# Two-item rounds in the paired attentions of a 13-stage fp32 model kernel on Trainium2

## The reference, cut to what matters

```python
def masked_softmax(s, mask):
    s = jnp.where(mask, s.astype(jnp.float32), -jnp.inf)
    m = jnp.max(s, axis=-1, keepdims=True)
    e = jnp.where(mask, jnp.exp(s - m), 0.0)
    return e / jnp.sum(e, axis=-1, keepdims=True)

# nsa, 16 query heads on 4 groups: per head a selected and a window branch over causal keys, each times a gate,
# plus a compressed branch; moba, 16 heads: one causal attention per head (256 tokens are one block)
s = jnp.einsum('bhqd,bhkd->bhqk', q, k)
o = jnp.einsum('bhqk,bhkd->bhqd', masked_softmax(s, causal), v)
# na, 16 heads: 256 latent queries over 256 context keys and the 256 latent keys, with a bias
p = jax.nn.softmax(jnp.concatenate([s_ctx, s_lat + bias], -1), axis=-1)
o = jnp.einsum('bqhd,bkhd->bhqd', p, v_all)
out = o.reshape(b, s, 1024) @ w_o
```

## Time and profile before

| | |
|---|---|
| median of 3 runs | 2262.74 us (2260.32 to 2263.0) |
| the profiled execution | 2257.97 us, span 2256.2 us, mean granted clock 0.994 |
| busy: TensorE, its weight loads | 98%, 88% |
| busy: VectorE, ScalarE | 79%, 52% |
| chain that ended last | TensorE 85%, VectorE 9%, ScalarE 3%, DMA 1% |
| `nsa0` from its first scores to the end of its output product | 91 to 148.5 us |
| `moba0` | 423 to 453.9 us |
| `nsa1` | 1019 to 1075.7 us |
| `na0` | 1974 to 2031.9 us |

### The profile page before, as it was taken

The page is one execution under the profiler, slowest core; times in us unless marked ns, Lnnn a source line. Parts: engine busy times, 40 slices in busy tenths (PEclk is TensorE's granted clock), DMA queues, the critical chain, the costliest instruction groups (busy, mean ns, idle before and its releaser), DMA issues.

```text
span 2256.2 us, 38067 instructions
## 1 busy us (share of the span) xinstructions
PE 2206.5 (98%) x15324; PEld 1975.6 (88%) x15324; DVE 1786.5 (79%) x3510; ACT 1162.2 (52%) x2042; POOL 0.2 (0%) x4
## 2 busy tenths in 40 slices
PE   8999999999999999999999999999999999999998
PEld 7878889898889988896988887898888889989998
DVE  7788977789887798878798766577877876478888
ACT  4685554665553555458655634544222136376433
POOL 0000000000000000000000000000000000000000
PEclk9999999999999999999999999999999999999999
DMA  7416666356665566660566532024554523334563
GB/s 244 141 61 222 234 203 222 124 190 235 204 212 187 190 236 204 213 204 35 206 233 205 178 115 91 1 76 142 175 177 157 170 81 109 133 101 155 209 225 122
DMA packets 70160, 373.60 MB, mean 166 GB/s; under 512 B 7392, under 2 KB 16736, under 8 KB 37984
## 3 DMA queue, kind: packets, MB, share of 16 engines
q1 hardware_dynamic: 61472, 361.52, 47.1%
q10 hardware_dynamic: 8512, 9.63, 1.4%
HBM read 369.03 MB, written 1.05 MB: 164 GB/s over the span
## 4 chain that ended last, share of the span: by engine, by line
PE 85%; DVE 9%; ACT 3%; DMA 1%; issue 1%; ACTq 0%; DVEq 0%
PE ps L490 82%; DVE w_lo L1874 2%; DVE hid_f L2279 1%; DVE hid_f L2264 1%; DMA w_raw<-weights 1%; PE ps L860 1%; PE ps L771 1%; PE ps L843 1%; ACT w_hi L1252 1%; ACT hid_f L1456 1%; DVE v_sb L2379 0%; DVE X L2000 0%; DVE X L2147 0%; PE ps L759 0%; DVE a_both L1874 0%
## 5 line engine op out<-in xcount | busy, mean ns | idle before, releaser
L490 PE MATMUL ps<-a_both,w_hi 128*128 128x256 f32 (+1 forms) x4864 | 1058.2, 328 | 16.0 <-DVE a_both L1931 10.5
L490 PEld LDWEIGHTS ps<-a_both,w_hi 128*128 128x128 f32 x4864 | 809.4, 190 | 90.1 <-issue 14.5
L1874 DVE TENSOR_TENSOR w_lo<-w_raw,w_hi 128x1024 fp32r<-128x1024 f32 (+1 forms) x632 | 708.0, 1149 | 92.4 <-ACT w_hi L1252 85.7
L490 PE MATMUL ps<-a_both,w_lo 128*128 128x256 f32 (+1 forms) x3136 | 715.2, 292 | 0.0
L1252 ACT CAST w_hi<-w_raw 128x1024 fp32r<-128x1024 f32 (+1 forms) x448 | 414.8, 974 | 379.7 <-DMA w_raw<-weights 372.8
L490 PEld LDWEIGHTS ps<-a_both,w_lo 128*128 128x128 f32 x3136 | 521.9, 191 | 24.0
L490 PE MATMUL ps<-hid_both,w_hi 128*128 128x512 f32 (+2 forms) x2216 | 529.0, 348 | 4.9 <-DVE qk L2845 0.8
L490 PEld LDWEIGHTS ps<-hid_both,w_hi 128*128 128x128 f32 x2216 | 381.9, 189 | 59.3 <-issue 9.8
L490 PE MATMUL ps<-hid_both,w_lo 128*128 128x256 f32 (+2 forms) x1460 | 340.5, 305 | 0.0
L490 PEld LDWEIGHTS ps<-hid_both,w_lo 128*128 128x128 f32 x1460 | 236.5, 190 | 16.9
L1258 ACT CAST w_hi<-w_raw 128x1024 fp32r<-128x1024 f32 (+2 forms) x184 | 188.3, 1023 | 0.8 <-DMA w_raw<-weights 0.8
(11 more groups left out here) (235 smaller groups left out, 1906.2 us busy)
## 6 DMA issues: line engine op xcount, KB each, us to landing
w_raw<-weights SPq DMA_DIRECT2D x250, 1024.0 KB, 4.8
pe_sb<-weights SPq DMA_DIRECT2D x96, 512.0 KB, 5.6
w_raw<-weights SPq DMA_DIRECT2D x64, 704.0 KB, 4.0
pe_sb<-na_bias ACTq DMA_DIRECT2D x32, 128.0 KB, 2.2
X<-x_t SPq DMA_DIRECT2D x2, 512.0 KB, 6.9
X<-c_rows ACTq DMA_DIRECT2D x2, 512.0 KB, 4.1
qk<-qk ACTq DMA_DIRECT2D x4, 256.0 KB, 6.8
qk<-ctx_t ACTq DMA_DIRECT2D x1, 1024.0 KB, 5.3
```

Source lines behind the costliest of these rows:

```text
L490: return nc.tensor.matmul(out, stationary, moving, start=start, stop=stop)
L1874: return v.tensor_tensor(out, a, b.bitcast(F32), ALU.subtract)
```

## The change

TensorE's loop goes by rounds of two items: scores of 2j and 2j+1, turn of 2j-2, values of 2j-4 and 2j-3, turn of 2j-1. ScalarE copies item i-2 at step i, and takes the high parts of a round together at odd steps, ahead of the copy; VectorE takes the low parts at even steps, of items i-6 and i-5. The output product's parts are cut at 5 and 6 tiles (at 3 and 5 in `moba0`). `moba0` has room for seven turned tiles. The steps themselves become functions (`pair_scores`, `pair_turn`, `pair_values`, `pair_exps`, `pair_copy`, `pair_high`, `pair_reduce`, `pair_normalize`, `pair_low`) with the old bodies; `ada_tile` gets an argument and `MOBA_S`, `MOBA_T`, `MOBA_O` are defined, neither of which is used.

```diff
-        PAIR_SLOTS = 3
+        PAIR_SLOTS, MOBA_TURNED = 3, 7
...
+        def turned_slots(name):
+            return MOBA_TURNED if name == "moba0" else PAIR_SLOTS
...
@@ TensorE, pair_attention @@
-                for i in range(N + 3):
-                    if i < N:
-                        if i >= 2:
-                            pe.wait_ge(a["s_taken"], i - 1)
...
-                    beside(i)
-                    if i == N:
-                        out_part(range(0, 3))
-                    b = i - 2
-                    if 0 <= b < N:
-                        pe.wait_ge(a["p_ready"], b + 1)
-                        wait(pe, a["t_taken"], b)
...
-                    if i == N + 1:
-                        out_part(range(3, 5))
-                    b = i - 3
-                    if 0 <= b < N:
...
-                out_part(range(5, KD))
+                def turn(b):
+                    pe.wait_ge(a["p_ready"], b + 1)
+                    wait(pe, a["t_taken"], b)
+                    pair_turn(name, b, PAIR_T)
...
+                first, second = (5, 6) if N == 2 * KD else (3, 5)
+                for j in range(N // 2):
+                    for i in (2 * j, 2 * j + 1):
+                        if j > 0:
+                            pe.wait_ge(a["s_taken"], i - 1)
+                        pair_scores(name, i, PAIR_S[i % 2])
+                        beside(i)
+                    if j > 0:
+                        turn(2 * j - 2)
+                    if j > 1:
+                        values(2 * j - 4, 2 * j - 3)
+                    if j > 0:
+                        turn(2 * j - 1)
+                out_part(range(0, first))
+                turn(N - 2)
+                values(N - 4, N - 3)
+                turn(N - 1)
+                out_part(range(first, second))
+                values(N - 2, N - 1)
+                out_part(range(second, KD))
...
@@ ScalarE, pair_attention @@
-                for i in range(N + 3):
+                for i in range(N + 4):
                     if i < N:
...
-                    b = i - 1
-                    if 0 <= b < N:
-                        act.wait_ge(a["t_ready"], b + 1)
-                        if b >= PAIR_SLOTS:
-                            act.wait_ge(a["pv_done"], b - PAIR_SLOTS + 1)
...
+                    if i % 2 == 1:
+                        for b in (i - 5, i - 4):
+                            if 0 <= b and items[b]["last"]:
+                                pair_high(name, b, PAIR_O)
+                    if 0 <= i - 2 < N:
+                        pair_copy(name, i - 2, PAIR_T)
                     if behind:
                         behind(i)
-                    b = i - 3
-                    if 0 <= b and items[b]["last"]:
...
@@ VectorE, pair_attention @@
-                for i in range(N + 4):
+                for i in range(N + 5):
...
-                    b = i - 4
-                    if 0 <= b and items[b]["last"]:
...
+                    if i % 2 == 0:
+                        for b in (i - 6, i - 5):
+                            if 0 <= b and items[b]["last"]:
+                                pair_low(name, items[b]["tile"], PAIR_O)
```

More of the change, by code:

```diff
@@ new lines, in pair_copy, with pair_high @@
+            def pair_copy(name, b, banks):
+                act.wait_ge(att[name]["t_ready"], b + 1)
+                if b >= turned_slots(name):
+                    act.wait_ge(att[name]["pv_done"], b - turned_slots(name) + 1)
+                turned = ps[:, banks[0]:banks[1] + 1, 0:WIDTH[name]].rearrange("p r (n c) -> p r n c", c=HD)
+                nc.scalar.copy(t_pair(name, b).rearrange("p (n r c) -> p r n c", r=2, c=HD), turned).then_inc(att[name]["t_taken"], 1)
+            def pair_high(name, b, banks):
+                act.wait_ge(att[name]["pv_done"], b + 1)
+                t = ITEMS[name][b]["tile"]
+                nc.scalar.copy(a_hi[:, t, LAT], ps[:, banks[t % 2], 0:S]).then_inc(att[name]["o_hi"], 1)
@@ L1444, in pair_attention @@
             def pair_attention(name, beside=None, behind=None, load_bias=None):
-                a, items = att[name], ITEMS[name]
-                N, W = len(items), WIDTH[name]
-                for i in range(N + 3):
+                items = ITEMS[name]
+                N = len(items)
+                for i in range(N + 4):
                     if i < N:
[L1450 to L1458, removed]
+                        pair_exps(name, i)
@@ new lines, in pair_reduce @@
+            def pair_reduce(name, i, banks, bias=False):
+                a, W = att[name], WIDTH[name]
+                dve.wait_ge(a["s_ready"], i + 1)
+                if i >= PAIR_SLOTS:
+                    dve.wait_ge(a["t_ready"], i - PAIR_SLOTS + 1)
+                rows = ITEMS[name][i]["rows"]
+                for e in range(2):
+                    slot = 2 * (i % 2) + e
+                    if bias:
+                        dve.wait_ge(bias_loaded[slot], 16 * (i // 2 + 1))
+                    for r, (c, mask) in enumerate(rows):
+                        x = len(rows) * e + r
+                        last = v.tensor_tensor_reduce(p_pair(name, i)[:, e * W + c.start:e * W + c.stop], ps[:, banks[e], c],
+                                                      bias_ring[:, slot, :] if bias else mask, NEG_SCALE[name], 3e38,
+                                                      ALU.add, ALU.min, negmax[:, i % 4, x:x + 1])
+                last.then_inc(a["s_taken"], 1)
@@ new lines, in pair_normalize @@
+            def pair_normalize(name, b):
+                a, W = att[name], WIDTH[name]
+                rows = ITEMS[name][b]["rows"]
+                w = 2 * len(rows)
+                g = ITEMS[name][b]["gate"]
+                dve.wait_ge(a["exp_done"], b + 1)
+                step(v.reciprocal(recip[:, b % 4, 0:w], sums[:, b % 4, 0:w]))
+                if g is not None:
+                    sync()
+                    both = recip[:, b % 4, :].rearrange("p (e r) -> p e r", e=2)
+                    step(v.tensor_tensor(both, both, gate[:, :, g:g + REP + 1:REP].rearrange("p r e -> p e r"), ALU.mult))
+                sync()
+                for e in range(2):
+                    for r, (c, _) in enumerate(rows):
+                        at = p_pair(name, b)[:, e * W + c.start:e * W + c.stop]
+                        x = len(rows) * e + r
+                        last = v.tensor_scalar(at, at, recip[:, b % 4, x:x + 1], None, ALU.mult)
+                last.then_inc(a["p_ready"], 1)
```

120 lines of the change are left out of this document (57 added, 63 removed).

## The result

| | before | after |
|---|---|---|
| median | 2262.51 us (2257.71 to 2263.0, 5 runs) | 2272.2 us (2270.98 to 2275.31, 5 runs) |
| profiled execution | 2257.97 us, span 2256.2 | 2275.31 us, span 2273.5 |
| mean granted clock | 0.994 | 0.991 |

Ratio 1.0053, 95% interval 1.0042 to 1.0064. By these ratios the change costs 12 and 16 us; the medians lie 9.7 and 13.8 us apart. The spans of the two profiled executions lie 17.3 us apart, 14.5 of it in the four paired attentions.

A forecast was written before the change was run, and what follows sets the result against it. In the paired attentions it took VectorE's pace, not TensorE, as nsa0's bound, and a new chain of waits as slower. nsa 3.0 + 3.0, na0 4.5, moba0 4.0, clock 1.5 make 16 us; forecast 2278 us, range 2266 to 2285.

The forecast's parts named there:

- The circle R, E, C, T, S, R: Paired attentions, per two items: reduction, exponentials, copy, turn, scores, next reduction; 5.40 us in nsa0, 5.56 in na0.
- Its length: Two items' chain of waits: 5.45 us against 5.31 in nsa0, 5.56 against 5.04 in na0; five rounds add 0.7, 2.6.
- T to S: From a turn to the next scores on TensorE, a link of the chain: 0.52 us in nsa0, 0.66 in na0.
- The start: Item 0's copy runs behind item 2's exponentials, delaying item 1's turn; item 4's reduction +0.95 us in nsa0.
- T13: Turn of item 13, whose shift is the stage's: +3.0 us in each nsa, +4.5 in na0.
- moba0: Paired attention of four rounds: later turns, then a 2 us wait for the third output tile's low part; +4.0 us.
- The clock: TensorE's idle time between the turns of items 0 and 1 may bring 1.2 GHz stretches: 1.5 us, bounds 0 and 5.8.
- The sum: 3.0 + 3.0 + 4.5 + 4.0 + 1.5 = 16 us on the profiled 2257.97, so 2274; forecast 2278 against the median.
- Lag only: Rival: rounds stay at 5.31 and 5.04 us, only the other shifts remain; 10.4 us, so 2273; chance 0.15.
- Shapes: Rival: TensorE's changes of array shape were the bound; 9.5 us gained, 2253, or 4.1 us, 2259; chance 0.08.
- Seven slots at nothing: Room in moba0 for seven turned tiles, where three were: costed at nothing.

The follow-up runs named there:

- e1: Changed kernel with ScalarE's copy of the turned tile back at its old place, one step earlier; 1.0022 of the time before.
- e2: Changed kernel with TensorE going item by item again in nsa and na, the late copy kept; 1.0170 of the time before.
- the filled hole: Changed kernel with ten throwaway matmuls between the turns of items 0 and 1 in each paired attention; 1.0053, again 1.0069 of the time before.
- e5: Changed kernel with even items' copies one step earlier, so both copies of a pair stand at odd steps; 1.0088 of the time before.
- e8: Changed kernel's TensorE rounds with all copies early in nsa and na, moba0 wholly in its old order; 0.9988 of the time before.
- e3: Changed kernel with three slots instead of seven for moba0's turned tiles; moba0 35.09 us, 1.0074 of the time before.
- e6: Changed kernel with odd items' copies one step earlier, so both copies of a pair stand at even steps; 1.0130 of the time before.
- e10: Changed kernel once more, unedited, in another comparison; 1.0069 of the time before.
- e12: Changed kernel with early copies in nsa and na, moba0 in old order, item 0's turn behind item 2's scores in na alone; 0.9991 of before.

## Why the prediction was right

The forecast was 2278 us, slower with 0.85; the runs gave 2272.2, inside the range. Both parts of the mechanism that was named are there, the circle of waits and the later start, but the rounds of the circle weigh about half of what was forecast. By its steps:

- **The circle R, E, C, T, S, R.** Right, shown by the links above, by e1 (undo the copy: the loss goes) and by e2 (lengthen the circle by V: 6.65 us). VectorE's R(2j) is released by the scores (0.56 us idle in `na0`; in `nsa0` 0.17 to 0.29 in some rounds and none in the others), and each turn starts 0.11 to 0.12 us behind a copy. That the trace would name ScalarE as its releaser was half right: the matmul rows of even turns do, the weight-load rows say "issue".
- **Its length.** Too long: 5.45 taken and 5.35 measured in `nsa0`, 5.56 and 5.41 in `na0`. The term that was mis-sized is T to S: 0.52 and 0.66 from the earlier trace rows, in the rounds 0.36 and 0.49. The weight loads of the turn took 0.61 us in the earlier trace rows and take 0.48 now, and the scores' loads start before they end. The other four links were right within 0.04 us. In `nsa0` every second round has R to E 0.2 longer, because ScalarE is still at C and H of the round before, so rounds of 5.26 and 5.48 take turns. In `nsa0` two items cost 0.04 more than before, not 0.14, in `na0` 0.37, not 0.52. From T3 to T13 that made 0.2 us in each `nsa` and 1.6 in `na0`, 2.0 together, where the sum had 4.1 for its rounds.
- **The start.** This is where most of the loss lies: T1 follows R0 by 12.95 us in `nsa0`, before by 9.89, and 1.0 of these 3.1 us is won back up to T3. T1 was put at 107.02 in `nsa0` and stands at 107.01. In `na0`, taking off the 11.0 us by which the stage starts later, 1990.77 was forecast and 1990.77 came.
- **T13.** Forecast 3.0 later in `nsa0`, measured 139.03 against 136.69, 2.3; in `na0` 4.5 against 4.2 (2034.83 - 11.0 = 2023.83 against 2019.66). The difference is mostly the rounds' length. That nothing changes behind T13 was right: 11.78 us from T13 to the `X` row against 11.85 in `nsa0`.
- **`moba0`.** Forecast +4.0 without the clock, measured +4.17, of which the filled hole takes back 1.0. The wait for the third tile's low part came, with 1.18 us instead of 2.
- **The clock.** Taken as 1.5 us between 0 and 5.8; from T0 to the last turns it was 3.1 in one execution and 4.5 in another, and not to be seen in the medians.
- **The sum.** 14.5 us without the clock were forecast, 11.4 (14.5 less 3.1) came in the profiled pair; with it 16 were forecast and 14.5 came. Some of that closeness is luck: the clock's term was 1.6 too low and stands against rounds and `moba0` that were taken too high. Against the medians, 10 to 14 us came instead of 16: the profiled execution of before lay 4.5 us below its median, and that of the change was the slowest of its five, 3.1 above.
- **The rivals.** *Lag only* gave 10.4 us and 2273, and the total can't tell it from the forecast. e1 can't either, since an early copy takes away the later start and the circle together. The rounds can: this rival wanted 5.31 and 5.04. In `nsa0` it is nearly right, with 5.35, and in `na0`, with 5.41, it is wrong. *Shapes* falls as the bound: e1 has the new order's changes of shape and gains 0.7 us in three stages, not 9.5. The stall itself is there: 0.17 us between V and S in e2, and 0.17 between V and T7 in e5, whose copy had ended 0.97 us earlier (121.83 + 0.80). The 0.2 us ahead of T7 and T13 in `na0` after the change are no measure of it, because those turns also wait for a copy.

The Trainium skill's rule (TensorEngine Tiling (Array Packing), Key Properties), that a change of the tiling mode drains the TensorE, names such a stall, and the traces agree with 0.17 us. By that rule alone the kernel would have gained; the measurement decides that fewer drains gain little where TensorE waits for another engine anyway (at most 2.3 us, in e8).

- **Seven slots at nothing.** Right (e3).

Open in part: why e1 and e8 run rounds 0.1 us shorter than before. The traces show a wait that went. In the kernel before, S10 stands behind T7 and V6 on TensorE, its matmuls end at 123.44, and R10 starts at 123.48. In e1 the scores S8 and S9 are both through at 119.17, and R8 starts at 119.43, as soon as VectorE is free. TensorE before and, second, in e1, with R8 in the third:

```profile
122.51 0.93 PE L490 MATMUL ps<-qk 64*128 64x128 f32 x8
```
```profile
117.23 1.94 PE L494 MATMUL ps<-qk 64*128 64x128 f32 x16
```
```profile
119.43 0.28 DVE L2296 CUSTOM_DVE_ANT_0 hid_f<-ps,sm 128x128 f32<-128x128 f32 x1
```

So scores side by side seem to be what the rounds on TensorE gain. No run shows it alone, since the order of the high parts changed with them.

## What to carry to other kernels

Before an engine's step is moved one place later, write down the circle that it closes with the single buffer it empties, in start-to-start times, and set it against the busiest engine's time for the same number of items; here 5.4 us against the 4.9 of e1 made 2.8 of the 4.4 us that the late copy cost `na0`, and the step that fell behind was the one that frees a lone buffer. Write down as well how much later the first step can start, since that is paid once in every stage: it made the rest in `na0` and most of the loss in the two `nsa`. Two hand-overs of one buffer should not stand next to each other in one queue; here that cost 0.8 to 1.0 us a round (e5, e6). And a reordering that suits stages with two items to an output tile has to be looked at again where each item ends one.

## What the runs showed of the hardware

- The same hole between T0 and T1 of `nsa0`, 3.40 us without a matmul, was followed by a clock of 1.00 throughout in one execution of the changed kernel, and by 0.50 for 7 us in another (e10, 107 to 114 us). From T0 to T15 the stage then takes 1.5 us more, with nothing changed in the code.
- Ten matmuls whose results are thrown away kept the granted clock at 1.00 behind all four holes, in both executions.
- Low clock comes ahead of the two `nsa` stages too, in every kernel of the study, also in the one before: 0.50 for some 7 to 14 us around R0. In the kernel before it fell at about 88 us, although TensorE had been busy for 2.00 of every 2 us from 76 us on. How far the low stretch reaches behind R0 moves T0 by up to 1.4 us (8.77 us behind R0 in e8's `nsa1`, 10.13 in e12's).
- Between a value product and the scores or the turn behind it TensorE's weight loads stood still for 0.17 us where nothing else was late (e2, e5).
